# Hybrid attention trunk in fp32: load order of modulation rows, slots and splits at first heads, query halves and rotation order

## The reference

```python
for l in range(DEPTH):                              # DEPTH = 2
    mod = (silu(c) @ w_mod[l] + b_mod[l])           # six rows of 1024; modc from c_ctx
    h = modulate(rms_norm(x), mod[0], mod[1])       # hc the same for the context
    p = h @ w_in[l]                                 # all branches' projections and gates
    y_ret = retention(rope(q), rope(k), v, g)       # 4 heads, key 128, value 256
    y_mla = attention(...)                          # 8 heads from normed ranks of 256
    y_gqa = attention(rope(norm(q)), rope(norm(k)), v)   # 8 query heads, 2 key heads of 128
    z = s(g0) * (y_ret @ w_ret_o) + s(g1) * (y_mla @ w_mla_o) + s(g2) * (y_gqa @ w_gqa_o)
    x = x + mod[2] * (z @ w_out[l])                 # s is the sigmoid
    h2 = modulate(rms_norm(x), mod[3], mod[4])
    x = x + mod[5] * (swiglu(h2, w_ffn_in[l]) @ w_ffn_out[l])
return rms_norm(x)
```

## Time and profile before

| | |
|---|---|
| median of 3 runs | 3534.91 us (3522.54 to 3536.19) |
| the profiled execution | 3530.96 us, its span 3528.8 |
| mean granted TensorE clock | 0.967 of full speed |
| TensorE | 3240.0 us busy (92%), 18760 matmuls |
| its weight loads | 2735.5 us (78%), beside the matmuls |
| VectorE | 1519.6 us (43%) |
| ScalarE | 1254.8 us (36%) |
| GpSimd | 397.4 us (11%) |
| DMA | 315.17 MB, 89 GB/s in the mean |

### The profile page before, as it was taken

The page is one execution under the profiler, slowest core; times in us unless marked ns, Lnnn a source line. Parts: engine busy times, 40 slices in busy tenths (PEclk is TensorE's granted clock), DMA queues, the critical chain, the costliest instruction groups (busy, mean ns, idle before and its releaser), DMA issues.

```text
span 3528.8 us, 49714 instructions
## 1 busy us (share of the span) xinstructions
PE 3240.0 (92%) x18760; PEld 2735.5 (78%) x18760; DVE 1519.6 (43%) x2047; ACT 1254.8 (36%) x1777; POOL 397.4 (11%) x304
## 2 busy tenths in 40 slices
PE   6999999999898889999999978998999898889998
PEld 5788877888777777788888867877777776668886
DVE  4555424445335533422222355553455445443333
ACT  3344432454333332211211234444355433432222
POOL 0011100111101201000100101110011101011001
PEclk9999999999999999999999999999999999999999
DMA  4222141111331143123142432222221232222222
GB/s 181 78 71 73 64 136 63 60 54 59 101 121 64 42 137 126 48 96 112 64 135 70 140 111 81 75 82 84 75 71 65 75 115 68 90 100 95 95 95 101
DMA packets 100921, 315.17 MB, mean 89 GB/s; under 512 B 11088, under 2 KB 21456, under 8 KB 100816
## 3 DMA queue, kind: packets, MB, share of 16 engines
q1 hardware_dynamic: 55872, 202.40, 17.2%
q10 hardware_dynamic: 44944, 111.32, 9.4%
HBM read 283.79 MB, written 29.88 MB: 89 GB/s over the span
## 4 chain that ended last, share of the span: by engine, by line
PE 45%; issue 8%; DVE 5%; ACT 2%; POOL 1%; DMA 1%; ACTq 0%; DVEq 0%; POOLq 0%
PE ps L1417 43%; PE ps L1531 1%; POOL ptl L1399 1%; DVE mx L927 1%; ACT wh L431 1%; PE ps L1509 1%; DVE wl L896 1%; DVE ptl L945 0%; DMA mraw<-in_wmod 0%; DVE tmp L906 0%; DVE tmp L1061 0%; DVE tmp L966 0%; ACT pth L484 0%; PE ps L1441 0%; ACT side L509 0%
## 5 line engine op out<-in xcount | busy, mean ns | idle before, releaser
L1417 PE MATMUL ps<-hh,wh 128*128 128x512 f32 x2768 | 827.2, 359 | 48.5 <-DVE wl L896 25.8
L1417 PE MATMUL ps<-hl,wh 128*128 128x512 f32 x2768 | 818.8, 356 | 0.0
L1417 PE MATMUL ps<-hh,wl 128*128 128x512 f32 x2768 | 815.5, 355 | 0.0
L896 DVE TENSOR_TENSOR wl<-raw,wh 128x1024 fp32r<-128x1024 f32 x364 | 484.1, 1330 | 645.6 <-ACT wh L431 616.1
L1417 PEld LDWEIGHTS ps<-hh,wh 128*128 128x128 f32 x2768 | 454.9, 191 | 138.3 <-issue 48.6
L1417 PEld LDWEIGHTS ps<-hh,wl 128*128 128x128 f32 x2768 | 455.6, 191 | 78.3
L1417 PEld LDWEIGHTS ps<-hl,wh 128*128 128x128 f32 x2768 | 455.0, 191 | 73.8 <-issue 0.7
L431 ACT ACTIVATE wh<-raw 128x1024 fp32r<-128x1024 f32 x364 | 382.5, 1051 | 228.7 <-PE ps L1417 193.2
L1417 PE MATMUL ps<-yh,wh 128*128 128x512 f32 (+1 forms) x1296 | 412.0, 372 | 27.5 <-DVE wl L896 15.1
L1417 PE MATMUL ps<-yl,wh 128*128 128x512 f32 (+1 forms) x1296 | 398.3, 362 | 0.0
L1417 PE MATMUL ps<-yh,wl 128*128 128x512 f32 (+1 forms) x1296 | 397.4, 361 | 0.0
(11 more groups left out here) (190 smaller groups left out, 3452.5 us busy)
## 6 DMA issues: line engine op xcount, KB each, us to landing
raw<-in_stream SPq DMA_DIRECT2D x364, 512.0 KB, 3.5
mraw<-in_wmod ACTq DMA_DIRECT2D x40, 512.0 KB, 3.5
prob<-in_wmod ACTq DMA_DIRECT2D x40, 512.0 KB, 3.5
gspill<-prob ACTq DMA_DIRECT2D x32, 384.0 KB, 2.3
tmp<-gspill ACTq DMA_DIRECT2D x24, 384.0 KB, 3.1
early_y<-in_wmod SPq DMA_DIRECT2D x12, 512.0 KB, 14.6
vraw<-gspill ACTq DMA_DIRECT2D x16, 384.0 KB, 3.5
dec<-in_dec ACTq DMA_DIRECT2D x8, 768.0 KB, 4.2
```

The source lines that it names most:

```text
L896: dve.tensor_tensor(wl[:, s, :], raw[:, s, :], wh[:, s, :].bitcast(F32), ALU.subtract).then_inc(sem("w_lo"), 1)
L1417: ins = pe.matmul(out, lhs[w], rhs[x](cols), start=start and n == 0, stop=stop and n == 2)
```

## The change

It has six parts, and leaves every product in place.

1. `first_load` issues the load of modulation row 0 of an `out` phase at the start of the `z` or `ffn` phase ahead of it, instead of at the start of `out`.
2. In the first turn of a begun merge, row 0 stands after the first half of chunk 1, fold 0 and row 1 after the second half, fold 1 at the turn's end.
3. `mla_in` ends with the splits of chunks 7 and 8. `mla_first` projects the query into slot 1 and the two held chunks into slots 0 and 1.
4. `gqa_in` splits chunk 2j+3 right after the reciprocal in both turns, chunk 5 too, ahead of the halves of the value; `gqa_first` has no split at its first tile.
5. With 512 tokens (layer 1) the query halves `qh` and `ql` are made at step 2 of the head before, not at step 3.
6. In retention TensorE's transposes no longer wait for `v_lo`, and VectorE rotates the query before it makes `vl`.

```diff
-        phase("mla_first", layer, 0, {}, total(head, head, HELD, *raws, attention(nq, first=1)), nt=nt)
+        phase("mla_first", layer, 0, {}, total(
+            head, head, HELD, {"free0": -1, "free1": 1}, *raws, attention(nq, first=1)), nt=nt)
...
-    for ph, after in zip(phases, phases[1:]):
+    for n, (ph, after) in enumerate(zip(phases, phases[1:])):
+        if ph["kind"] in ("z", "ffn"):
+            ph["out"] = next(x for x in phases[n:] if x["kind"] == "out")
...
+                qslot = 0 if held_at is None else 1
...
-                        act.activation(tmp[:, 0, 0:nt], pair(0)[:, 0:nt], ACT.Copy).then_inc(sem("free0"), 1)
+                        act.activation(tmp[:, 0, 0:nt], pair(qslot)[:, 0:nt], ACT.Copy).then_inc(sem(f"free{qslot}"), 1)
                     for j, steps in enumerate(pieces):
-                        if n == steps[0]:
+                        if n == steps[0] and not (qslot and j == 0):
...
-                    if query and n == 0:
+                    if query and n == 0 and held_at is None:
                         split(at, c0 + 1)
...
-                    if query and n == 3:
+                    if query and n == (3 if nt > LAT else 2):
                         act.wait_ge(sem("v_full"), at.v("v_full", kq + 1))
                         act.activation(queries[par][0][:, 0:nt], tmp[:, 0, 0:nt], ACT.Copy).then_inc(
                             sem("v_hi"), 1)
...
+            def first_load(ph):
+
+                if ph["nmod"]:
+                    mod_load(ph, 0, ph["j0"] + ph["home"] * N_MOD * KT)
...
-                    roped(at, 5, 4, 0, 0, kh, P, MLA_NOPE, TOK, before=lambda: split(at, 7))
+                    def ahead():
+                        split(at, 7)
+                        split(at, 8)
+                    roped(at, 5, 4, 0, 0, kh, P, MLA_NOPE, TOK, before=ahead)
...
-                        if j == 0:
-                            split(at, 3)
+                        split(at, 2 * j + 3)
...
                 elif kind == "z":
+                    first_load(ph["out"])
...
-                            mod_load(ph, 0, row0)
...
                 elif kind == "ffn":
+                    first_load(ph["out"])
...
+                        roped(t, (0, 0), 0, 0, 1, qh, ql, 0, nt)
                         dve.wait_ge(sem("vt_hi"), t.v("vt_hi", 1))
                         dve.tensor_tensor(vl_f[:, :], ps[:, 5 * BANK:8 * BANK], vh_f[:, :].bitcast(F32),
                                           ALU.subtract).then_inc(sem("vt_lo"), 1)
-                        roped(t, (0, 0), 0, 0, 1, qh, ql, 0, nt)
...
-                        project(at, c0, 0, f0, R[0], RKT, nt, whole)
+                        project(at, c0, 1 if alone else 0, f0, R[0], RKT, nt, whole)
                     for j, steps in enumerate(pieces):
-                        gate(at, c0 + query + j, j if alone else f0 + query + j, steps, n, widths[j],
-                             1 - j if alone else 0)
...
                                 if ph["nmod"] and begun:
                                     if k == 1:
-                                        mod_fold(t, r)
-                                    if k != r:
-                                        mod_row(t, k, ph)
+                                        if r:
+                                            mod_fold(t, 0)
+                                        mod_row(t, r, ph)
                                 elif ph["nmod"]:
                                     mod_fold(t, k) if r else mod_row(t, k, ph)
+                        if ph["nmod"] and begun:
+                            mod_fold(t, 1)
...
-                        pe.wait_ge(sem("v_lo"), t.v("v_lo"))
```

More of the change, by code:

```diff
@@ L492, in y_hi, with spill @@
                                ACT.Copy).then_inc(sem("y_hi"), 1)
-            def spill(at, kc, f, kg, nt, full, held_at, skip):
-                slot = 1 if held_at is not None and kg == 0 else 0
+            def spill(at, kc, f, kg, nt, full, slot, held_at, skip):
                 act.wait_ge(sem("product"), at.v("chunk", kc + 1))
@@ L530, in fill @@
                             spill(at, c0 + query + j, f0 + query + j if held_at is None else j, kg + j,
-                                  widths[j], nt > LAT,
+                                  widths[j], nt > LAT, j if qslot else 0,
                                   None if held_at is None else held_at + j, skip)
@@ L572, in fill @@
                             spill(at, c0 + query + j, f0 + query + j if held_at is None else j, kg + j,
-                                  nt, nt > LAT,
+                                  nt, nt > LAT, 0 if held_at is None else 1 - j,
                                   None if held_at is None else held_at + j, skip)
@@ L694, in _ @@
                     head, scale = heads(ph)
-                    c1, f1, h0 = (4, 4, 0) if kind == "mla_first" else (3, 2, 2)
+                    c1, f1, h0 = (4, 3, 0) if kind == "mla_first" else (3, 2, 2)
                     fill = head(at, 0, 0, 0, 0, 0, held_at=RET_HEADS * layer + h0)
@@ L982, in mla_head @@
                 q, pieces, k, v = mla_steps(nt // P, raws)
+                qslot = 1 if alone else 0
                 def fill(n):
@@ L987, in fill @@
                     if query and n == q + 1:
-                        dve.wait_ge(sem("free0"), at.v("free0", f0 + 1))
+                        dve.wait_ge(sem(f"free{qslot}"), at.v(f"free{qslot}", f0 + 1))
                         cosine(at, MLA_NOPE)
@@ L1008, in fill @@
                 def fill(n):
-                    if query and n == 0:
+                    if query and n == 0 and not alone:
                         split(at, c0 + 1)
@@ L1165, in _ @@
                     head, scale = heads(ph)
-                    c1, f1 = (4, 4) if kind == "mla_first" else (3, 2)
+                    c1, f1 = (4, 3) if kind == "mla_first" else (3, 2)
                     fill = head(at, 0, 0, 0, 0, 0, alone=True)
@@ L1557, in mla_head @@
                 q, pieces, k, v = mla_steps(nt // P, raws)
-                ck, fk = c0 + 1 + raws, f0 + (2 if alone else 1 + raws)
+                ck, fk = c0 + 1 + raws, f0 + (1 if alone else 1 + raws)
                 s = at.slot(ck)
@@ L1563, in fill @@
                     if query and n == q:
-                        project(at, c0, 0, f0, R[0], RKT, nt, whole)
+                        project(at, c0, 1 if alone else 0, f0, R[0], RKT, nt, whole)
                     for j, steps in enumerate(pieces):
-                        gate(at, c0 + query + j, j if alone else f0 + query + j, steps, n, widths[j],
-                             1 - j if alone else 0)
+                        gate(at, c0 + query + j, j if alone else f0 + query + j, steps, n, widths[j], j if alone else 0)
                     if query and n == k:
```

## The result

| | before | changed |
|---|---|---|
| median | 3530.35 us (4 runs, 3522.54 to 3536.19) | 3487.61 us (4 runs, 3480.62 to 3489.99) |
| ratio of the runs | | 0.9877, 95% interval 0.985 to 0.9904 |
| the profiled execution | 3530.96 us, span 3528.8 | 3480.62 us, span 3478.5 |
| mean granted clock | 0.967 | 0.974 |

The account below looks back on a forecast made before the run. TensorE, busy 3240.0 of 3528.8 us, was taken as the bound, so only its 288.8 us idle and half-speed stretches could shrink. Terms summed to 44.9 us off the profiled 3530.96, giving 3486; forecast 3487, range 3466 to 3508.

Parts of the forecast that it names:

- first `out`: Layer 0's first `out`: the 6.29 us `mraw` wait goes, chunk 1's split then comes last; 7.4 us gained.
- three `ffn` outs: The `ffn` outs: row waits of 0.64, 0.60 and 1.71 us go whole; 2.9 us gained.
- begun merges: Two begun merges: first gains nothing, second starts 1.8 us earlier, each starts chunk 2 1.5 us later; together -1.3 us.
- `mla_first`, layer 1: Layer 1's `mla_first`: chunk 8 no longer waits for its split, key projection starts earlier; 5.6 us gained.
- `gqa_first`, layer 1: Layer 1's `gqa_first`: chunk 5 starts at 2525.7 instead of 2530.50, set by the halves of `vl`; 4.9 us gained.
- query halves: Layer-1 heads, step 2: 0.6 us in six heads, 1.0 lost in the seventh, plus some clock; 4.1 us gained.
- retention, layer 1: Layer 1's retention heads: rotating first takes 1.76 us of `vl` out of the key copy's chain; 6.8 us gained.
- The wait behind the named one: At each edited place, whatever comes last without the named wait sets the edit's value; the named wait is only its ceiling.
- The rival in which the named waits vanish whole: All edited places: the ceilings add up to 65 us, giving 3466 us; chance 0.12.
- one stretch had been credited: Layer-1 heads: of three lower-clock stretches behind waits, some 1.5 us each, only one was counted as saved.
- keeps the gain: Layer 1's `gqa_first`: the next chunk's split, 1.2 us later by its place, would leave the 4.9 us intact.
- Nothing else is due there: The three `ffn` outs: no second wait would follow the removed row waits, so 2.9 us is gained.

Follow-up runs that it names:

- The filled heads: Kernel before with 8, then 3, overwritten extra matmuls ahead of TensorE's `ql`/`q2l` wait in six layer-1 heads; 3530.85 and 3530.15 us against 3533.07, ratio 0.9996 both.

## Why the forecast held, term by term

The table has the time of each place in traces without the part and in traces with it (means; in brackets how many traces).

| place | forecast | without | with | gain |
|---|---|---|---|---|
| first `out` | 7.4 | 21.0 (6) | 15.2 (4) | 5.8 |
| three `ffn` outs | 2.9 | 41.0 (6) | 38.6 (7) | 2.4 |
| begun merges | -1.3 | 119.1 + 99.9 (8) | 121.4 + 100.3 (2) | -2.7 |
| `mla_first`, layer 1 | 5.6 | 36.0 (6) | 30.8 (7) | 5.2 |
| `mla_first`, layer 0 | 1.7 | 46.6 (6) | 44.7 (7) | 1.9 |
| `gqa_first`, layer 1 | 4.9 | 39.9 (6) | 35.8 (7) | 4.0 |
| `gqa_first`, layer 0 | 6.9 | 25.0 (6) | 18.2 (7) | 6.7 |
| query halves | 4.1 | 215.0 (4) | 207.6 (4) | 7.4 |
| retention, layer 0 | 5.9 | 189.5 (5) | 183.2 (3) | 6.3 |
| retention, layer 1 | 6.8 | 169.0 (5) | 162.2 (3) | 6.8 |

The gains add up to 43.8. By the medians the change gave 42.7 in the first series and 40.8 in the second (3530.72 less 3489.95); 44.9 were forecast. The forecast held because each term was right within 3.3 us, and the errors have both signs. That the sum came within 2 to 4 us is in part luck: the query halves gave 3.3 more than forecast, and six other terms together 5.0 less.

- **The wait behind the named one set each value.** The split at the first `out` (1.8 us, forecast 1.3), `wl` behind the query of `mla_first`, `ptl` and `side` in the heads (0.8 each, 0.9 forecast for the first), `kl` in layer 1 (2.4, forecast 2.5) all stood where the forecast put them. The rival in which the named waits vanish whole, 65 us, is out.
- **Query halves, forecast 4.1, measured 7.4: the term that was most mis-sized.** The handoffs gave 0.6 a head as worked out. What was mis-sized is the clock: three of six heads took 33 us in every one of the four traces without the edit, and none in the four with it, where one stretch had been credited. The Trainium skill (TensorE: Matmul & The Clock Gate, Part 1), by which an array left idle drops to half rate, had given 7.1, and the trace agrees: all three stretches went. The filled heads show that it was the idle.
- **Begun merges, forecast -1.3, measured -2.7.** Chunk 2 of the first merge comes the forecast 1.5 us later behind chunk 1, clock aside. What the step left out is that the row's matmuls had broken a wait in two: without them the 3.21 us are unbroken, and in one of the two traces the half projection behind them takes 5.9 us instead of 4.2. That trace lost 4.8 at the two merges, the other 0.7.
- **First `out`, forecast 7.4, measured 5.8**, 6.9 in the first pair. The four traces with the early load spread from 13.7 to 17.5 us: the wait for the split is 1.2 to 3.1 us as the clock ahead of it varies, and behind it the lower clock came in two of them.
- **`gqa_first` in layer 1, 0.9 short**: "keeps the gain" was wrong, as the faster projection runs into the next split. **`mla_first` in layer 1, 0.4 short**; which handoff took it was not tested.
- **The `ffn` outs, forecast 2.9, measured 2.4.** "Nothing else is due there" was wrong for the last of them: in all seven traces with the early load row 1 is waited for there, 0.9 to 1.4 us. It is the forecast's own rule, missed at one place: a second wait stood behind the named one.
- **Retention, forecast 12.7, measured 13.1.** The mechanism is as given: `yl` no longer waits, `kl` waits 2.4, and the two halves of the edit are worth less one by one. The near hit of layer 1, 6.8 for 6.8, is luck: it is reached only with the two slow traces in the mean. Against the three at 166.8 to 167.0, the kernel before among them, the edit gave some 4.8. The waits for `yl` and `kl` did shrink by 6.7, but those for `ptl`, which the term left out, are 0.1 to 1.7 longer in the three traces with the edit than in the kernel before, and the rest is clock.

## What to carry to other kernels

When a wait is to be removed, ask in the same rows what comes last without it; the edit is worth the distance to that, and an order that loses today can win once the other input is early, as the rows of the merges did. In a kernel like this count a TensorE wait with what the clock loses behind it: where a wait of 2.3 us was shortened or broken, 1.6 us of the lower clock went in every second head, whether or not the wait itself was won. Check terms of a few microseconds place by place over several traces, since one execution's time does not resolve them.

## What the runs showed of the hardware

**Waits and the clock.** In the thirteen traces there are 1507 waits of TensorE of 0.5 us and more that began at the full clock. Counted by the granted clock are those behind which, within 8 us and before the next such wait, over 1 us was spent at the lower level (matmul starts about twice as far apart: 0.64 us instead of 0.35 for 768 columns, 0.43 instead of 0.23 for 512). Of 1036 waits under 2.0 us it was 84; of 156 between 2.0 and 2.5 us, 96; of 315 longer ones, 259. These are counts over unlike places, and what else differs between them is not held fixed. It is not all chance: of the six heads behind like waits in layer 1, 2.3 to 2.45 us long, it was three in each of the four traces, nearly always every second one. At other places it does vary; the same wait of 2.82 us before the retention phase was followed by the full clock in the kernel before and by the lower one in the changed kernel (a pair of matmuls took 0.61 and 1.00).

**Two paces at full clock.** Dense stretches whose granted clock reads 1.00 ran at two paces. The kernel before and the changed one in the same stretch of `ffn`, from one pair of matmuls to the 24th behind it:

```profile
1480.97 0.51 PE L1417 MATMUL ps<-hh,wh 128*128 128x512 f32 x2
...
1489.45 0.51 PE L1417 MATMUL ps<-hh,wh 128*128 128x512 f32 x2
```

```profile
1459.38 0.51 PE L1430 MATMUL ps<-hh,wh 128*128 128x512 f32 x2
...
1467.70 0.51 PE L1430 MATMUL ps<-hh,wh 128*128 128x512 f32 x2
```

That is 0.353 and 0.347 us a pair. Both paces appear in kernels with and without the change, and some traces go from one to the other once or twice, so it is not the change's. Over the three stretches between the outs of the `ffn` the first pair of traces differs by 6.1 us (582.7 and 576.6), with as much time at the lower clock in both. That is most of the 6.5 by which their spans differ beyond the sum of the table. What sets it stays open.
